# Merge, output projection, norm and queries divided at token 256, the last 320 tokens' part moved into the groups of tile 0's expert rows

## The reference, cut to what matters

```python
wb = w_branch[l]
merged = (gates[:, :, 0] * (o_a @ wb[:512])
          + gates[:, :, 1] * (o_b @ wb[512:768])
          + gates[:, :, 2] * (o_c @ wb[768:]))          # gates: sigmoid of logits
x = x + merged @ w_out[l]
x = x + _peer(_rmsnorm(x, norm_ffn[l]), ...)

def _peer(h, w_query, subkeys, w_up, w_down):           # 8 heads, 2 x 128 keys, top 16
    q = h @ w_query                                     # 1024 -> 2048 = 16 units of 128
    s = q . subkeys                                     # (token, head, 2, 128)
    expert, gate = top 16 of the 16 x 16 best pairs of each head, softmax
    act = gelu(h . w_up[expert]) * gate                 # 128 expert rows for each token
    return sum(act * w_down[expert])                    # 16384 experts in the table
```

## Time and profile before

| | us |
|---|---|
| median of 3 runs | 5066.31 (5065.96 to 5066.34) |
| the profiled execution | 5062.91 |
| its span, first to last instruction | 5061.1 |
| TensorE busy | 3929.1 (78%) |
| VectorE busy | 3048.1 (60%) |
| ScalarE busy | 1160.5 (23%) |
| GpSimd busy | 1594.9 (32%) |
| mean granted TensorE clock | 0.871 |

### The profile page before, as it was taken

How to read it: one execution, slowest core, us unless ns; L and a number is a source line. 1 busy time by engine, 2 the same in 40 slices (tenths; PEclk the granted TensorE clock), 3 DMA queues, 4 the chain that set the end, 5 groups by cost and what they waited for, 6 DMA issues and landing times. The chain is left out here.

```text
span 5061.1 us, 59054 instructions
## 1 busy us (share of the span) xinstructions
PE 3929.1 (78%) x21640; PEld 2181.7 (43%) x21640; DVE 3048.1 (60%) x7335; ACT 1160.5 (23%) x3105; POOL 1594.9 (32%) x1418
## 2 busy tenths in 40 slices
PE   8899999998855555589998897799887565555555
PEld 6766677754411111134475776776542111111111
DVE  6523323247889898754446644432777999985555
ACT  2211211113322222221121223110322222221111
POOL 0412000014444444443330342100344444444443
PEclk9999999999977777789998999999998767777777
DMA  2223232339999999999993234441999999999998
GB/s 110 84 73 119 73 132 96 129 129 409 411 395 420 419 417 414 411 419 419 416 415 140 84 108 166 170 166 39 377 412 407 397 419 415 419 412 416 420 413 349
DMA packets 266402, 1473.00 MB, mean 291 GB/s; under 512 B 27008, under 2 KB 77952, under 8 KB 113600
## 3 DMA queue, kind: packets, MB, share of 16 engines
q0 software_dynamic: 176608, 1263.35, 61.3%
q1 hardware_dynamic: 79168, 198.75, 10.7%
q10 hardware_dynamic: 10336, 7.12, 0.5%
HBM read 1433.90 MB, written 55.34 MB: 294 GB/s over the span
## 5 line engine op out<-in xcount | busy, mean ns | idle before, releaser
L2986 PE MATMUL ps<-early,diag 64*64 64x512 f32 x6912 | 1128.1, 782 | 671.5 <-ACT diag L2925 664.1
L2814 POOL DMA_INDIRECT early<-in_peer,ids x964 | 1112.0, 1153 | 1427.5 <-PE ps L2986 1104.8
L2847 DVE SCALAR_TENSOR_TENSOR early<-early,rows 128x1024 f32<-128x1024 f32 x964 | 1165.2, 1223 | 519.2 <-DMA early<-in_peer,ids 509.3
L2986 PEld LDWEIGHTS ps<-early,diag 64*64 64x64 f32 x6912 | 270.7, 161 | 1457.4 <-ACT diag L2925 1046.4
L2925 ACT ACTIVATE diag<-consts_sb,weight 128x64 f32<-128x64 f32 x1152 | 338.0, 340 | 736.8 <-DVE weight L2861 725.0
L1336 PE MATMUL ps<-hT,gate_ring 128*128 128x288 f32 (+2 forms) x1728 | 464.9, 423 | 7.3 <-ACT gate_out L1348 3.4
L2917 ACT ACTIVATE gel<-dot 128x2 f32<-128x2 f32 x576 | 117.2, 203 | 1326.1 <-DVE early L2847 1083.0
L1336 PEld LDWEIGHTS ps<-hT,gate_ring 128*128 128x128 f32 x1728 | 314.6, 192 | 154.3 <-issue 43.2
L2986 PE MATMUL ps<-late,diag 64*64 64x512 f32 x1152 | 210.7, 866 | 151.6 <-ACT diag L2925 151.6
L2814 POOL DMA_INDIRECT late<-in_peer,ids x172 | 198.0, 1151 | 270.2 <-PE ps L2986 199.5
L2847 DVE SCALAR_TENSOR_TENSOR late<-late,rows 128x1024 f32<-128x1024 f32 x172 | 208.1, 1223 | 107.2 <-DMA late<-in_peer,ids 105.0
(11 more groups left out here) (392 smaller groups left out, 5813.7 us busy)
## 6 DMA issues: line engine op xcount, KB each, us to landing
gate_ring<-in_in_gate POOLq DMA_DIRECT2D x48, 512.0 KB, 4.1
slot<-in_w_branch SPq DMA_DIRECT2D x16, 1152.0 KB, 5.2
ring<-in_in_delta SPq DMA_DIRECT2D x8, 2048.0 KB, 9.2
early<-in_peer,ids POOLq DMA_INDIRECT x964
slot<-gate_rows SPq DMA_DIRECT2D x16, 864.0 KB, 7.1
slot<-in_in_pool SPq DMA_DIRECT2D x6, 2048.0 KB, 10.4
late<-in_peer_query SPq DMA_DIRECT2D x24, 512.0 KB, 7.9
gate_ring<-in_in_gate SPq DMA_DIRECT2D x24, 512.0 KB
```

Of the source, the lines that this page charges most:

```text
L2814: pool.indirect_dma_start(place(q), None, table_rows, bass.IndirectOffsetOnAxis(ap=ids[:, n, c:c + 1], axis=0)).then_inc(s.pair[PLACE[q]], 16)
L2847: nc.vector.scalar_tensor_tensor(out=up, in0=up, scalar=1.0, in1=rows[:, n, :], op0=ALU.mult, op1=ALU.mult, accum_out=dot[:, i % 2, k:k + ...
L2986: last = nc.tensor.matmul(g.ps[k * NS:(k + 1) * NS, SUM_BANK[n] + 2 * r + m, :], diag[half, q % DIAGS, :], place(q)[half, D + m * 512:D + ...
```

## The change

The merge, the output projection, the norm, the transposes and the queries are divided at token 256. Tiles 0 and 1 stay ahead of the expert rows; tiles 2, 3 and 4 (320 tokens) go into the groups of tile 0.

- `Output` now has 256 columns and the order 0, 1. Its first four query units are loaded ahead into places 6 and 7. `first_queries`, `first_scores` and `first_route` follow tile 1.
- A new class `Rest` holds the last 320 tokens. SyncE copies their columns of `oa`, `ob`, `oc` to other places of SBUF (`move`). Unit m of 24 has its weights and gate logits loaded again, through a ring of three; units 0 and 1 stand ahead of group 0, unit m in group m - 2. `w_out` is loaded again after the last unit, the output projection stands in groups 26, 28, 30, 32 and 34, gamma is loaded again, squares, mean, root, rows and transposes stand in groups 32 to 44.
- Near queries use one buffer, a unit each four groups; far queries (320 tokens) stand in groups 48, 50, ... 78 with all 16 units' weights loaded a second time, their scores two groups later.
- Gathers start after tiles 0 and 1 are normed, with no further wait up to pair 5; pairs 6 and 7 wait for the four first query units. A place is used again after 8 pairs up to pair 203 (`EXTENDED = 204`), after 10 from there. The places in `MIXED` are gone. Tile 1's sums use tile 0's banks, and wait for its fold.

Core of the diff ("..." marks what is left out):

```diff
 class Output:
-    ORDER = (4, 0, 1, 2, 3)
+    ORDER = (0, 1)
...
-            if u >= 2:
-                pe.wait_ge(s.branch_read, u - 1)
+            if u >= 4:
+                pe.wait_ge(s.branch_read, u - 3)
...
-                w = merge.weights(j)[:, k0 + k, :]
-                nc.tensor.matmul(g.ps[:, u % 2, 0:HALF], w, self.src[b][:, k, 0:HALF], start=k == 0, stop=k == nk - 1)
-                last = nc.tensor.matmul(g.ps[:, 2 + u % 2, 0:HALF], w, self.src[b][:, k, HALF:TOK], start=k == 0, stop=k == nk - 1)
+                last = nc.tensor.matmul(g.ps[:, u % 4, 0:NEAR], merge.weights(j)[:, k0 + k, :], self.src[b][:, k, 0:NEAR],
+                                        start=k == 0, stop=k == nk - 1)
...
+            if n == 0:
+                dve.wait_ge(s.loaded2, 16)
+                dve.wait_ge(s.rest_moved, 48)
...
+REST_FIRST = 2
+REST_AT = {m - REST_FIRST: m for m in range(REST_FIRST, len(REST_UNITS))}
+OUT_UNITS = ((2, 0), (3, 0), (2, 1), (3, 1), (4, None))
+OUT_AT = {26 + 2 * v: v for v in range(len(OUT_UNITS))}
...
+class Rest:
...
+    def load(self, sp, m):
...
+        if m >= REST_RING:
+            sp.wait_ge(s.branch_sum, MERGE_UNITS + m - REST_RING + 1)
+            sp.wait_ge(s.branch_read, MERGE_UNITS + m - REST_RING + 1)
...
+        sp.dma_start(self.weights(m), self.merge.w_b[j][:, k0:k0 + nk, :]).then_inc(sem, 16)
+        sp.dma_start(self.gate(m), self.merge.logits[3 * j + b][:, NEAR:TOK]).then_inc(sem, 16)
...
+    def open(self, act, m):
...
+        self.nc.scalar.activation(self.gate(m), self.gate(m), ACT.Sigmoid).then_inc(s.gate_open, 1)
+
+    def read(self, dve, link, m):
...
+        dve.wait_ge(s.gate_open, KT + m + 1)
+        dve.wait_ge(s.branch_sum, MERGE_UNITS + m + 1)
...
+        if b == 0:
+            nc.vector.tensor_tensor(to, self.gate(m), bank, ALU.mult).then_inc(s.branch_read, 1)
+            return
+        link(nc.vector.tensor_tensor(self.gate(m), self.gate(m), bank, ALU.mult))
...
+        nc.vector.tensor_tensor(to, to, self.gate(m), ALU.add).then_inc(s.branch_read, 1)
...
+    def vector_first(self, dve, link, i):
...
+        if i - 1 in REST_AT:
+            self.read(dve, link, REST_AT[i - 1])
+        if i - 1 in OUT_AT:
...
+            dve.wait_ge(s.out_sum, 2 * NEAR_TILES + v + 1)
...
-EXTENDED = 154
-Q_RING = 4
+EXTENDED = 204
+FIRST_UNITS = 4
+ASKED = {1: ("query", 4), 3: ("scores", 4), 5: ("query", 5), 7: ("scores", 5)}
+FAR_AT = 48
...
@@ VectorE's loop over the groups
             for i, (n, c0) in enumerate(BY_GROUP):
...
+                rest.vector_first(dve, link, i)
                 for k in range(GROUP):
...
+                rest.vector(dve, link, i)
                 following.vector(dve, link, i)
@@ ScalarE's loop
                 if i:
                     for kind, u, a in asking[i - 1]:
                         ask(kind, u, a)
+                rest.scalar(act, i)
@@ TensorE's loop
                 for kind, u, a in asking[i]:
                     ask(kind, u, a)
+                rest.tensor(pe, i)
                 following.tensor(pe, i)
                 pe.wait_ge(s.diagonal, (i + 1) * GROUP)
@@ GpSimd's loop
-                    if q == FREE_FIRST:
-                        pool.wait_ge(s.out_sum, 2 * TILES)
+                    if q == 0:
+                        pool.wait_ge(s.out_sum, 2 * len(out.ORDER))
+                        pool.wait_ge(s.normed, len(out.ORDER))
+                    if q == 6:
+                        pool.wait_ge(s.pe_a, FIRST_UNITS)
```

More of the change, by code:

```diff
@@ L2372, in vector, with __init__ @@
                                            op0=ALU.mult, op1=ALU.mult).then_inc(s.normed, 1)
-        self.turned(dve, nc.vector.tensor_copy, self.ORDER[-1], 1)
+        if i in TURN_AT:
+            self.turned(dve, nc.vector.tensor_copy, TURN_AT[i], 1)
 class Late:
[L2379 to L2388, removed]
+    def __init__(self, g, sb):
+        self.places = g.space(AT_LATE)("late", [P, LATE, 2 * D])
+        near = g.space(AT_NEAR)
+        self.sc1, self.keysT = near("sc1", [P, NQ, KEYS]), near("keysT", [P, 2, P])
+        self.hT = g.space(AT_HEAD_T)("head_t", [P, KT, NEAR])
+        self.far_hT = g.space(AT_MERGED)("far_t", [P, KT, FAR])
+        far = g.space(AT_MIX)
+        self.far_sc = far("far_sc", [P, NQ, len(FAR_TILES), KEYS])
+        single = sb("single", [P, KT, P])
+        self.near_units = g.space(AT_WORK + 6 * 2 * D)("first_units", [P, FIRST_UNITS, KT, P])
+        self.single = single
+        self.far_units = [single, far("far_unit", [P, KT, P]), g.space(AT_MOVED)("far_unit", [P, KT, P])]
@@ L2749, in last_tensor, with score_expert_stage @@
                 self.turn(pe, LAST_TILE, a).then_inc(s.next_turned, 1)
-def score_expert_stage(nc, g, t, l, rows, sc, sc0, ids, gates, router, late, w_q, out, sb, following):
+def score_expert_stage(nc, g, t, l, rows, sc0, ids, gates, router, late, w_q, out, rest, sb, following):
     s = g.s
@@ L2839, in _ @@
             out.vector(dve, link, first_route)
+            for m in range(REST_FIRST):
+                rest.read(dve, link, m)
             for i, (n, c0) in enumerate(BY_GROUP):
@@ L2902, in ask @@
                     scores(u, a)
[L2904 to L2909 removed]
+            out.scalar(act)
+            first_queries()
+            first_scores()
+            out.turned(act, nc.scalar.copy, 1, 0)
+            out.turned(act, nc.scalar.copy, 1, 1)
+            for u in range(FIRST_UNITS):
+                query(u, 0)
+                if u < REST_FIRST:
+                    rest.open(act, u)
+                scores(u, 0)
             router.gate_exp(act, 0, 0)
[L2911 to L2912 removed]
             for i, (n, c0) in enumerate(BY_GROUP):
@@ L2935, in query @@
             def query(u, a):
-                i, c = halves.index((u, a)), columns(u, a)
-                if a == 0:
-                    pe.wait_ge(unit_ring[u % Q_RING], 16 * (u // Q_RING + 1))
-                if i >= 2:
-                    pe.wait_ge(s.act_a, i - 1)
+                if a:
+                    pe.wait_ge(s.far_units[u % FAR_RING], 16 + 16 * (u // FAR_RING + 1))
+                    if u >= 2:
+                        pe.wait_ge(s.act_a, NQ + u - 1)
+                    else:
+                        pe.wait_ge(s.hT_a, NEAR_TILES + len(FAR_TILES))
+                        pe.wait_ge(s.hT_b, NEAR_TILES + len(FAR_TILES))
+                    for k in range(KT):
+                        last = nc.tensor.matmul(g.ps[:, 4 + u % 2, 0:FAR], late.far_units[u % FAR_RING][:, k, :], late.far_hT[:, k, :],
+                                                start=k == 0, stop=k == KT - 1)
+                    last.then_inc(s.pe_a, 1)
+                    return
```

490 lines of the change are left out of this document (312 added, 178 removed).

## The result

The changed kernel takes 5111.07 us (median of 5, 5098.71 to 5119.48), the kernel before 5066.31. The ratio is 1.0083, interval 1.0065 to 1.0100: slower by 0.8%, 42 us by the ratio and 45 by the medians, where +14 was forecast.

The account below looks back on a forecast made before the run. TensorE was taken to bound the head, DMA bytes the expert rows. Start -101, bytes +64, time not full +43 and later groups +1 made +7 us a layer, +14 in all: 5080 us, range 5015 to 5132.

Parts of the forecast that it names:

- Start: Head of a layer: first gathers near 1000, DMA engines full from about 1002 instead of 1102.9; -101 us a layer.
- The loop: Groups 1 to 21: VectorE's read waits for ScalarE's Sigmoid, 3.6 us more a group; 169 us, plus 7 for clock.
- `w_out`: Second load ahead of the far projection: issued at about 1192, shares the engines with the gathers, lands in 20 us.
- Time not full: Tile 0's groups up to 35: DMA engines move 252 us of work in 295; +43 us a layer.
- The projections themselves: Far projection groups: each pair of groups is a chain of 16.1 or 14.5 us, where the DMA engines need 10.3.
- Bytes: Loads added while gathers run: 43.8 us of weights, gates and gamma, 20.5 of query units; +64 us a layer.
- some 30 MB more a layer: Sign for the added loads: the DMA traffic of each layer grows by some 30 MB.
- After group 36: Later groups: small parts, far queries fit; fold wait and 8 places may cost 3, old stop saves 2; +1 us.
- Rival 1: Gather groups: engines stay full, only some 8 us start-up loss; 5010, half of it 5045; together chance 0.28.
- Rival 2: Groups 0 to 35: TensorE's lower clock, about 0.75, makes it the bound; +28 us a layer, 5136; chance 0.15.
- Rival 3: Groups with far units: table change costs twice its row on the chain; 27 us a layer, 5134; chance 0.05.
- Rival 4: Head of a layer: copies or near loads hold it by 10 us a layer; 5100; chance 0.04.

Follow-up runs that it names:

- the Copy run: Changed kernel with the far gates opened by a Copy in place of the Sigmoid (far results wrong): 5095.12 us, ratio 1.0063.
- The 4 KB run: Changed kernel with w_out's second load cut by rows, in runs of 4 KB in place of 2 KB: 5082.62 us, ratio 1.0040.
- the later projection: Changed kernel with far projection, norm, transposes and far queries six groups later: 5063.27 us, ratio 0.9998.
- their run: Kernel before with 8 places until pair 203, in place of 153 (EXTENDED 154 made 204): 5081.86 us, ratio 1.0031.

## Why the prediction was right, and where its terms were off

**Start: right.** First gather 997.3, worked out 999.9; the 2.4 us between them are the mixing part's, since the merge began at 888.8 and not at 891.2. From the merge on it is 108.5 us in place of 202.7, 94.2 less, where 94.0 was worked out. By the same reckoning as for the earlier trace rows, 15 us at 0.91 from 997 on make the engines full from 998.5 in place of 1102.9: -104 us, forecast -101. Doubling it was a little too much: layer 1 has 6 us less, in the mixing part.

**The loop: right in its time and, for 17 groups of 21, in its cause.** Groups 0 to 21 took 169.5 us, the working had 169 and 7 more for TensorE and its clock, which didn't come. VectorE waited ahead of the read in each of the 21 groups: 17 times for the Sigmoid, 43.8 us, which is 2.6 a group as worked out, and 4 times for TensorE's product, 16.5 us, all four for units of 12 blocks. Beyond the 2.6 that the Sigmoid would have cost there anyway, the product added 6 us, and the working had 3 us twice. What it didn't see is how close behind the Sigmoid the product stands in the other groups: the Copy run took 33 us of waits for ScalarE away and got 24 of waits for the product in their place. What holds both ways is the place of the read, and moving it gave 25 us a layer in these groups. The DMA engines' floor of 6.8 us a group was right: 144.6 / 21 = 6.9 at a share of 1.01.

**`w_out`: the term that was mis-sized.** The step that was off is "shares the engines with the gathers: 20 us", about an equal share. It was 38.9 us (4.19 MB, so 108 GB/s beside gathers), and TensorE began at 1227.8, not 1212. From there to the sums of group 35 the working had 85 us (1212 to 1297); it took 82 to its weight at 1310.1 and some 3 more to the sums, 85 again. The 16 us a layer of that one landing, 32 in all, are most of the distance from 5080 to 5111. The 4 KB run and the later projection show the cause from two sides: 22 and 43 us came back.

**Time not full: the sum was near by luck.** Up to group 35, from the table of stretches: 0.09 x 168 + 0.04 x 32 + 0.09 x 16 + 0.39 x 82 = 50 us (1.01 less the share, by length) and 1.5 before 1012, where 43 stood. But the working had about 35 of the 43 in the loop (176 us less 21 x 6.8 / 1.01) and 8 behind it, and the trace has 15 in the loop and 35 behind it. In the loop the share read 0.92 and not 0.85, in part because two more gathers moved there, and in part because the gathers' packets took longer: by the shares of the queues, 117.5 us for 46.0 MB, 2.55 us a MB, where the same groups with the read behind the dots have 108.6 us for 44.3 MB, 2.45. Two errors, of some 20 and 27 us, nearly cancelled. The projections themselves were nearly right: the weights of two groups in a row lie 16.2 to 17.3 us apart, where 14.5 to 16.1 stood, and 5 us for the clock.

**Bytes: right to a few us.** The hardware queue's time rose from 0.107 x 5061 to 0.134 x 5111 us, 143 for 51.0 MB, so 2.81 us a MB and not 2.67 (the two shares are rounded, so this is good to 0.1): the 24.3 MB cost 68 a layer in engine time, where 64 stood over a ceiling of 1.01. The sign "some 30 MB more a layer" was off, at 25.5: the far gates were moved and not added. A term was left out: the gathers moved the same 1263.35 MB, but their packets took 15 us more in all (0.610 x 5111 against 0.613 x 5061), 7 a layer. With the read behind the dots this is gone (3101 us in all before, 3117 after, 3101 in that run).

**After group 36: +1 was too little, by some 5 us.** Groups 35 to 102 took 22 us a layer more (371.6 against 349.9), but most of this is already in the bytes' term: there the hardware queue moved 9.7 MB where it had moved 1.3, and took 21 us more, while the gathers took 6 us less. With shares of 0.986 and 1.001, the time not full rose by 6 us. The places were cleared by their run. How the 6 us divide between TensorE's queue and the lost slack stays open.

**The layer closed.** From the first gather to the last weight, both layers take 118.6 us more. At a ceiling of 1.012 that is 63 and 66 us of the hardware queue's time, 7 of the gathers' packets, and 50 and 46 us not full. The first gather comes 97 and 91 us earlier, counted from the end of the layer before. That leaves 22 and 28 us, the 50 by which the spans of the two profiled executions differ.

**Rivals.** Rival 1 fell: the DMA share in the first 300 us of the gathers was 0.84. Rival 2 fell: the clock was 0.91 in the groups with far units, and of the stretches in the table only the 16 us in which TensorE had nothing to do read 0.50. Rival 3 fell with the rows: 46 Sigmoid loads at 1.28 us each, each starting within 0.02 us of the end of what came before. Rival 4 fell with the start. The drain of about 1.38 us of the Trainium skill, "ScalarE: Activation LUTs", "What ACT_TABLE_LOAD costs", shows in none of these; the trace disagrees with it here. Sigmoid and Gelu do stand in different sets, as the same page of the Trainium skill says under "Table sets: the hidden batching unit": the trace has a load for each way in each group with a far unit.

## What to carry to other kernels

When work is interleaved into a pipelined loop, ask where each new wait stands in its engine's queue, not only how much work it brings: a read that waits for two other engines belongs behind the work whose inputs are already there. A lead that is won in the head is lent, and every us in which the bounding resource is not full pays it back; add these up stretch by stretch. And a bulk load that must meet a point in a saturated stretch needs its landing time taken from a row of the same run length beside the same traffic, not from its bytes; and its first user should wait for the part that it reads, not for the whole.

## What the runs showed that I had not expected

Beside gathers in runs of 8 KB, 4.19 MB landed after 37 to 41 us in runs of 2 KB and after 25 to 28 us in runs of 4 KB, with the same total bytes and the same three transfers: of these two lengths the shorter one got the smaller share. A stall costs more than its length. TensorE, left without work for 16 us at a clock of 0.50, ran its next projection in 8.74 us at a mean clock of 0.81, and the one after in 7.49 at 0.95, where the third took 7.1 at 1.00. And where the stream of gathers is broken up their packets take longer: in groups 27 to 35, at a share of 0.73, 2.67 us a MB of engine time, where the kernel before has 2.45 there. So a DMA share below its ceiling shows less than the whole loss.
